# Attention scores of two heads: from six products over 64 rows to two over 128 rows and two over 64

## What is computed

```
def gqa_attention(q, k, v):
    scale = HEAD_DIM ** -0.5
    def attend(qb):
        s = jnp.einsum('bqkgd,bskd->bkgqs', qb, k).astype(jnp.float32) * scale
        p = jax.nn.softmax(s, axis=-1).astype(v.dtype)
        return jnp.einsum('bkgqs,bskd->bqkgd', p, v)
```

## Time and profile before

| | us |
|---|---|
| median of 3 executions | 1592.58 |
| lowest and highest of them | 1592.32, 1596.58 |
| the profiled execution, its own time | 1590.77 |
| its span, first instruction to last | 1589.4 |
| PE matmuls busy in the span | 1533.3 |
| DVE busy | 878.1 |
| ACT busy | 637.2 |

### The profile page before, as it was taken

One profiled execution on the slowest core, in us unless ns is written; L12 is line 12 of the kernel. 1 busy time (PEld: TensorE's weight loads), 2 busy tenths in 40 slices (PEclk: granted clock), 3 DMA queues, 4 the chain that ended last, 5 costly groups with the idle time before them and its releaser, 6 DMA issues.

```text
span 1589.4 us, 24518 instructions
## 1 busy us (share of the span) xinstructions
PE 1533.3 (96%) x10213; PEld 1311.1 (82%) x10213; DVE 878.1 (55%) x1589; ACT 637.2 (40%) x1134; POOL 48.6 (3%) x50
## 2 busy tenths in 40 slices
PE   7999999999999999999999899999999998999997
PEld 5888866778888888898988679999988987678886
DVE  4435666666635656866554554447665544554443
ACT  6242275544313344734343542223433343542333
POOL 0000010000000000020000000000110000000000
PEclk9999999999999999999999999999999999999999
DMA  7324200052333332431213002233431213013231
GB/s 257 106 58 107 66 2 28 24 148 81 105 103 84 106 105 81 104 70 54 75 33 80 28 28 80 81 100 127 80 80 54 60 48 81 14 44 116 80 120 53
DMA packets 166399, 125.13 MB, mean 79 GB/s; under 512 B 46608, under 2 KB 161296, under 8 KB 166288
## 3 DMA queue, kind: packets, MB, share of 16 engines
q1 hardware_dynamic: 166288, 123.56, 26.7%
HBM read 121.45 MB, written 2.10 MB: 78 GB/s over the span
## 4 chain that ended last, share of the span: by engine, by line
PE 87%; DVE 5%; ACT 5%; issue 2%; DMA 1%; SPq 1%; POOL 0%; DVEq 0%; ACTq 0%; POOLq 0%
PE bank L601 70%; PE bank L2802 2%; PE bank L2766 2%; PE bank L2782 2%; PE bank L3182 1%; PE bank L2669 1%; DVE w_lo L542 1%; PE bank L1641 1%; ACT w_hi L533 1%; PE bank L1583 1%; PE bank L3143 1%; ACT probs L1513 1%; PE bank L1459 1%; PE bank L3161 1%; DMA x_rows<-x 1%
## 5 line engine op out<-in xcount | busy, mean ns | idle before, releaser
L601 PE MATMUL bank<-h_hi,w_hi 128*128 128x512 f32 (+2 forms) x920 | 323.4, 371 | 12.7 <-DVE h_lo L791 7.5
L542 DVE TENSOR_TENSOR w_lo<-w_raw,w_hi 128x2048 fp32r<-128x2048 f32 (+2 forms) x116 | 238.8, 2059 | 172.9 <-ACT w_hi L533 172.3
L601 PE MATMUL bank<-h_hi,w_lo 128*128 128x512 f32 (+2 forms) x920 | 317.1, 365 | 0.0
L601 PE MATMUL bank<-h_lo,w_hi 128*128 128x512 f32 (+2 forms) x920 | 316.9, 364 | 0.0
L533 ACT ACTIVATE w_hi<-w_raw 128x2048 fp32r<-128x2048 f32 (+2 forms) x116 | 199.1, 1717 | 69.1 <-DMA w_raw<-w_in 29.9
L601 PEld LDWEIGHTS bank<-h_hi,w_hi 128*128 128x128 f32 (+1 forms) x920 | 165.4, 188 | 48.2 <-issue 18.0
L601 PEld LDWEIGHTS bank<-h_hi,w_lo 128*128 128x128 f32 (+1 forms) x920 | 165.2, 188 | 28.3
L601 PEld LDWEIGHTS bank<-h_lo,w_hi 128*128 128x128 f32 (+1 forms) x920 | 165.3, 188 | 26.8 <-issue 0.5
L601 PE MATMUL bank<-g_hi,w_hi 128*128 128x264 f32 (+1 forms) x752 | 181.2, 307 | 1.5 <-DVE z_a L2198 0.9
L601 PE MATMUL bank<-g_hi,w_lo 128*128 128x264 f32 (+1 forms) x752 | 178.7, 303 | 0.0
L601 PE MATMUL bank<-g_lo,w_hi 128*128 128x264 f32 (+1 forms) x752 | 178.6, 303 | 0.0
(11 more groups left out here) (594 smaller groups left out, 2573.5 us busy)
## 6 DMA issues: line engine op xcount, KB each, us to landing
w_raw<-w_in SPq DMA_DIRECT2D x44, 1024.0 KB, 5.2
w_raw<-w_up SPq DMA_DIRECT2D x32, 512.0 KB, 4.9
w_raw<-w_in SPq DMA_DIRECT2D x40, 256.0 KB, 4.4
w_raw<-w_down SPq DMA_DIRECT2D x8, 1024.0 KB, 5.0
w_raw<-w_out SPq DMA_DIRECT2D x8, 1024.0 KB, 5.0
w_raw<-w_out SPq DMA_DIRECT2D x8, 512.0 KB, 3.5
w_raw<-w_ple_gate SPq DMA_DIRECT2D x4, 1024.0 KB, 5.0
w_raw<-w_o_attn SPq DMA_DIRECT2D x8, 512.0 KB, 3.4
```

The lines of the kernel that those rows point to most:

```text
L542: DV.e.tensor_tensor(wlo[u % RING][:, 0:n], raw[u % RING][:, 0:n], whi[u % RING][:, 0:n].bitcast(F32), ALU.subtract).then_inc(*w_low(u))
L601: ins = PE.e.matmul(out, stationary[a](k), moving[b](k)[i], start=first and n == 0, stop=last and n == 2)
```

## The change

The queries and keys are laid out so that the high and the low part of one head stand above each other in the 128 partitions. `q_both[g]` has the high part of group g on that group's own half and the low part on the other half. `k_twin[g]` has the high part of group g's keys on both halves. One product over all 128 rows then gives high by high plus low by high. The third term, high by low, stays a product over 64 rows.

```
-                    for n, (q_, k_) in enumerate(((y.q_hi, y.k_hi), (y.q_hi, y.k_lo), (y.q_lo, y.k_hi))):
-                        for g in range(2):
-                            rows = slice(AD * g, AD * g + AD)
-                            ins = PE.e.matmul(bank[:, 2 + g, :], q_[rows, x // 2, t * P:(t + 1) * P], k_[rows, :],
-                                              start=n == 0, stop=n == 2)
-                            if n == 2:
-                                ins.then_inc(*g_scored(l, i + g))
+                    queries = [q_[:, x // 2, t * P:(t + 1) * P] for q_ in y.q_both]
+                    for g in range(2):
+                        PE.e.matmul(bank[:, 2 + g, :], queries[g], y.k_twin[g][:, :], start=True, stop=False)
+                    for g in range(2):
+                        rows = halves_of[g]
+                        PE.e.matmul(bank[:, 2 + g, :], queries[g][rows, :], y.k_lo[rows, :], start=False,
+                                    stop=True).then_inc(*g_scored(l, i + g))
```

The parts are made half by half, `halves_of[g]` being partitions 64g to 64g + 63:

```
         def ac_query_high(l, j):
-            AC.e.activation(y.q_hi[:, j, 0:S], y.qT[:, j, 0:S], ACT.Copy).then_inc(*h_high("q", l, j))
+            for g in range(2):
+                ins = AC.e.activation(y.q_both[g][halves_of[g], j, :], y.qT[halves_of[g], j, 0:S], ACT.Copy)
+            ins.then_inc(*h_high("q", l, j))
         def dv_query_low(l, j):
-            DV.e.tensor_tensor(y.q_lo[:, j, 0:S], y.qT[:, j, 0:S], y.q_hi[:, j, 0:S].bitcast(F32),
-                               ALU.subtract).then_inc(*h_low_d("q", l, j))
+            for g in range(2):
+                ins = DV.e.tensor_tensor(y.q_both[g][halves_of[1 - g], j, :], y.qT[halves_of[g], j, 0:S],
+                                         y.q_both[g][halves_of[g], j, :].bitcast(F32), ALU.subtract)
+            ins.then_inc(*h_low_d("q", l, j))
         def ac_key_high(l):
-            AC.e.activation(y.k_hi[:, :], y.kT[:, 0:S], ACT.Copy).then_inc(*h_high("q", l, "k"))
+            for g in range(2):
+                for to in (g, 1 - g):
+                    ins = AC.e.activation(y.k_twin[g][halves_of[to], :], y.kT[halves_of[g], 0:S], ACT.Copy)
+            ins.then_inc(*h_high("q", l, "k"))
         def dv_key_low(l):
-            DV.e.tensor_tensor(y.k_lo[:, :], y.kT[:, 0:S], y.k_hi[:, :].bitcast(F32), ALU.subtract).then_inc(*h_low_d("q", l, "k"))
+            for g in range(2):
+                rows = halves_of[g]
+                ins = DV.e.tensor_tensor(y.k_lo[rows, :], y.kT[rows, 0:S], y.k_twin[g][rows, :].bitcast(F32), ALU.subtract)
+            ins.then_inc(*h_low_d("q", l, "k"))
```

More of the change, by code:

```diff
@@ L375, in program @@
             assert c <= (g_end if y.last else g_at)
-            y.q_hi, y.q_lo = [place(f"q_{n}_{L}", [P, 4, ROW], F32R, g_at_of[l] + 16 * ROW * i)[0]
-                              for i, n in enumerate(("hi", "lo"))]
+            y.q_both, c = [None] * 2, g_at_of[l]
+            for g in range(2):
+                y.q_both[g], c = place(f"q_both{g}_{L}", [P, 4, S], F32R, c)
+            twin, _ = place(f"k_twin1_{L}", [P, S], F32R, c)
             y.qT, c = place(f"q_{L}", [P, 4, T2], F32, R)
@@ L401, in program @@
             c += (P - c) % (2 * P)
-            y.k_hi, c = place(f"k_hi_{L}", [P, S], F32R, c)
+            k_twin, c = place(f"k_twin0_{L}", [P, S], F32R, c)
+            y.k_twin = (k_twin, twin)
             y.k_lo, c = place(f"k_lo_{L}", [P, S], F32R, c)
@@ L2331, in dv_scaled_keys @@
                              y.ks[:, 1, TT, :].unsqueeze(2).broadcast_to([P, 2, AD])).then_inc(*k_wide(l))
+        halves_of = [slice(g * AD, (g + 1) * AD) for g in range(2)]
         def ac_query_high(l, j):
```

## The result

| | before, us | after, us |
|---|---|---|
| median of 5 executions each | 1592.47 | 1600.55 |
| lowest and highest | 1590.72, 1596.58 | 1599.42, 1602.08 |
| the profiled execution | 1590.77 | 1600.55 |
| its span | 1589.4 | 1599.2 |

The ratio is 1.0053 [1.0041, 1.0066]: the changed kernel is slower by 0.53%, 8.1 us in the medians and 9.8 us between the two profiled executions. The forecast was 1598.2 us in a range of 1591.0 to 1603.5. The way and the range hold; the sum, +5.6 us, was too small, and one of its parts was missing.

A forecast was written before the change was run, and what follows sets the result against it. The prediction took PE's queue to bound the kernel. It added 3.4 us in the groups and 2.2 us at the starts, +5.6 us on a median of 1592.58, for 1598.2 us in a range of 1591.0 to 1603.5.

The forecast's parts named there:

- What bounds the kernel: Stage gqa, both layers: PE's queue moves the end; DVE or ACT time counts only where PE waits for them.
- The removed third: Score groups: products on different array halves run side by side, so three slots before and after; fewer matmuls save nothing.
- The groups: PE, score groups: one more shape change at 0.21 us in 8 of 16 groups per layer, +3.4 us in all.
- the sign to look for: Group behind value products: steps of 0.34, 0.33 and 0.44 us, 1.11 us in all where it was 0.90.
- the switch inside costs nothing: Rival, score groups: 14 entry switches go, -2.9 + 2.2 = -0.7 us, 1591.9 us; chance 0.22.
- the one with switches at 0.36 us: Rival, groups and starts: both dearer, +10.1 to +11.3 us, 1602.7 to 1603.9 us; chance 0.18.
- the one by the count of matmuls: Rival, score groups: cost goes by number of matmuls, 4 for 6, -6.8 us, 1585.8 us; chance 0.05.
- The start: Half-row splits on ACT and DVE ahead of the meta scores lengthen PE's wait in each layer, +2.2 us in all.
- the term of 1.12 us a layer: PE's wait for the meta scores: 0.52 us from the last query split plus 0.60 from the keys' low part.
- the bound of 3.4: Upper end for the longer meta-score wait, 2 x (1.12 + 0.60) us, if half-row operations writing the other half are dearer.
- The sum: Whole kernel: 3.4 us in the groups plus 2.2 us at the starts, +5.6 us.
- The dear case: Rival, groups and starts: switches and starts both dearer, +10.1 to +11.3 us, 1602.7 to 1603.9 us; chance 0.18.

The follow-up runs named there:

- e10: Kernel before with all six products of a group on the lower half of the array, so the second head gets the first's scores; 1611.28 us, ratio 1.0126.
- e7: Kernel before with three more copies on ACT ahead of the last query split, so PE waits longer for the meta scores; 1597.43 us, ratio 1.0036.
- e9: Kernel before with two more copies on ACT ahead of the last query split; 1595.28 us, ratio 1.002.
- e4: Changed kernel with the meta copy ahead of the last query split on ACT and the keys' low part earlier on DVE; 1595.46 us, ratio 1.0023.
- e5: Kernel before with the meta copy ahead of the last query split on ACT and the keys' low part earlier on DVE; 1590.26 us, ratio 0.9988.
- e1: Kernel before, its six matmuls kept, with the high and low parts made half by half as in the change; 1596.48 us, ratio 1.0033.
- e3: Kernel before with the same six matmuls ordered by head, three on the lower half, then three on the upper; 1592.82 us, ratio 1.0006.
- e11: Changed kernel with meta copy and keys' low part moved earlier, and the pair made two more products over 128 rows; 1590.07 us, ratio 0.9985.
- e2: Changed kernel with the pair over 64 rows ahead of the two full products; 1597.38 us, ratio 1.0041.
- e6: Kernel before with one more copy on ACT ahead of the last query split; 1593.91 us, ratio 1.0015.

## Why the prediction was right or wrong

**What bounds the kernel: right.** Every microsecond in the table of shifts is on PE's queue.

**The removed third was free: right**, and shown by e10.

**The groups: right in size, 3.4 against 3.3.** Step by step the sign to look for was 0.34, 0.33 and 0.44 us, 1.11 in all; the group took 0.66 and 0.43, 1.09. Behind transposes the term was 0, and the trace gives 1.43 us for 1.43. The turns grew by 1.56 and 1.78 us, against 8 x 0.21 = 1.7 a layer. The Trainium skill's rule on weight loads (TensorE: Matmul & The Clock Gate, What happens when you issue a matmul), by which the pair's load would have been hidden, does not hold across this change of shape: PEld stood idle for 0.36 us ahead of it. So does the rival fall by which the switch inside costs nothing, as does the one with switches at 0.36 us, and the one by the count of matmuls, which e10 and the change itself contradict.

**The start: the mechanism right, the term of 1.12 us a layer too small.** "So each half costs the full 0.52 us" and "+0.60 us" took the distance between two neighbouring operations for the price of one more. Measured, the last query part takes 1.28 us to the next start instead of 0.52, +0.76, and the keys' part 1.41 instead of 0.60, +0.81. That is 1.57 us a layer in both layers, 3.1 in all, where 2.2 stood; the bound of 3.4 held it, though it was meant for a crossing that costs next to nothing. The distance is shorter than the operation because operations over 128 partitions overlap: before, `q_own` starts at 721.39, 0.09 us ahead of the end of `q_hi` at 720.87 + 0.61. What follows an operation over 64 partitions starts 0.01 to 0.03 us behind its end, as `q_own` at 723.12 behind 721.84 + 1.25. So two halves cost their two whole durations, 0.61 and 0.63 us on ACT, 0.67 and 0.69 on DVE. The row cited for the price had this in it: two copies over 64 partitions take 0.43 us, more than twice the 0.18 of one over 128.

**The step that was missing.** The prediction charged PE's longer wait at its own length: "Nothing is between it and the fill behind it in PE's queue". That is so, but the fill itself became slower: behind the wait, which reached 2.8 us and not 2.3, the granted clock fell to 1.2 GHz for most of 4 us, which cost 1.6 us in each layer, 3.2 in all. e7 and e9 show that a longer wait alone can do it, and e4 and e5 that without the wait it does not happen there. The row for it was in the trace of the kernel before, which I had read only in the stages of the change, where the clock is 1.00. Early in the program, in lines that the change doesn't touch, PE waits 2.19 us. The timeline there, and a window behind it, of the kernel before:

```profile
298.70 1.04 PE L1576 MATMUL bank<-identity,probs 128*32 128x128 f32 x4 [2.19 <-ACT branch_factor L1541]
...
301.57 0.60 PE L601 MATMUL bank<-h_hi,w_hi 128*128 128x512 f32 x1
```

```profile
300.00:304.00 4.00, 4.00 (x26) 3.29 (x23) 3.74 (x19) 4.00 (x18) 0.00 (x0) 0.77 0.00 0
```

The same lines in e1, behind the same wait:

```profile
298.36 0.61 PE L1576 MATMUL bank<-identity,probs 128*32 128x128 f32 x4 [2.19 <-ACT branch_factor L1541]
...
299.93 0.50 PE L601 MATMUL bank<-h_hi,w_hi 128*128 128x512 f32 x1
```

```profile
300.00:304.00 4.00, 3.82 (x20) 3.03 (x20) 3.46 (x18) 3.78 (x17) 0.00 (x0) 1.00 0.00 0
```

From the transposes to the fill it is 301.57 - 298.70 = 2.87 us with the clock down, and 299.93 - 298.36 = 1.57 with it up: a wait of 2.2 us can cost 1.3 us behind it, in one execution and not in another. In the same trace of before the clock stayed up behind a wait of 1.86 us at 339.6 us. A wait forecast to reach 2.3 us should have carried a term of 0 to 1.3 us for that in each layer.

**The sum.** By the stretches the profiled executions differ by 3.15 us at the starts, 3.18 by the clock, 3.34 in the groups and 0.17 ahead of the first stage gqa, 9.8 us in all; 5.6 was forecast. The medians differ by 8.1, since the profiled execution of before is 1.7 us below its median and that of after is at its own. Between the two profiled executions the clock is the larger part of the error, 3.2 of 4.2 us, and the start 0.9. In the medians the error is 2.5 us; how it divides one profile of each doesn't tell.

**The rivals and the range.** The dear case gave 1602.7 to 1603.9 us by a mechanism that isn't there, and the time came within 2.2 us of it by another. That the range held owes something to that case.

## What to carry to other kernels

A wait that grows on a busy TensorE costs more than its length where the clock falls behind it, so a term "PE waits x us longer" needs a second one, read from another place in the trace where PE waited as long, and given as a range, since one place shows only what happened once. On the array, count slots and changes of shape, not matmuls: two half-height products are one slot, and each change of shape lays a load and an emptying open, here 0.2 us. An operation split in two over 64 partitions on ACT or DVE costs two whole durations on a chain, where the single one cost only the distance to the next start: here 0.76 and 0.81 us more, not 0.52 and 0.60.

## What the runs showed that was not expected

**The halves of the array don't wait for each other's order in the code.** In e3's code three matmuls of the lower half are ahead of the three of the upper, and they still start in pairs, 0.34 and 0.23 us apart, 0.90 us a group. The Trainium skill (TensorE: Matmul & The Clock Gate, What happens when you issue a matmul) has the matmuls themselves stay in program order and only the loads pulled ahead; by that the group would be five slots. The measurement decides: 1592.82 us, ratio 1.0006 [0.9997, 1.0016]. The trace lists products by their start, not by their place in the queue, so it doesn't show whether the engine or the translation of the program brings the pairs together; in e11 the products start in the order of the code.

**The clock after a wait is not settled by the wait.** Ahead of the meta transposes it fell behind ten of the eleven waits of 1.8 to 3.0 us, and behind none that was shorter. Elsewhere it is otherwise. Behind one and the same wait of 2.19 us early in the program it fell in four of the thirteen profiled executions (before, after, e5 and e7) and stayed up in nine. Behind the wait of 1.86 us at some 340 us it fell in seven of them. Behind the first long wait of stage na, 1.50 us in either layer, it fell in 5 of 26 cases, and once or twice each it fell behind waits of 1.1 to 1.2 us (e4 above; e2, e3 and e6 before 300 us). A case of stage na, in e5:

```profile
885.41 0.60 PE L3142 MATMUL bank<-na_mask,ident 128*128 128x384 bf16 x2 [1.50 <-DVE attn_stats_a L3301]
```

```profile
886.00:890.00 4.00, 3.71 (x20) 2.77 (x19) 1.90 (x12) 2.19 (x11) 0.00 (x0) 0.61 0.00 0
```

So a kernel with such waits has more than one time, and its executions show it: of the 27 of the kernel before that stand beside e11, the one with a mean granted clock of 0.998 took 1589.0 us, the four with 0.993 took 1594.9 to 1595.9. The executions of e6, whose waits in stage gqa are 2.0 and 1.3 us, spread over 5.4 us (1591.34 to 1596.70), those of e5, which has none there, over 1.9.

**What stays open.** What settles whether the clock falls behind a wait of 1 to 2.3 us (in e2 it fell once, at some 1169 us, with no wait at all ahead: PE was busy, with eight products of 2 columns, four of 128, one of 16 and ten of 1), and how often it does so at each place: with one profile of each kernel the medians can't be divided among the places.
